# The half-swap of a rotary embedding: four ScalarE copies between partition groups in place of a matmul with a constant

## The reference

```
def _rotary(x, pos):
    half = x.shape[-1] // 2
    inv = ROPE_BASE ** (-jnp.arange(half, dtype=jnp.float32) / half)
    ang = pos.astype(jnp.float32)[:, None] * inv[None, :]
    cos = jnp.cos(ang)[None, :, None, :]
    sin = jnp.sin(ang)[None, :, None, :]
    xf = x.astype(jnp.float32)
    x1, x2 = xf[..., :half], xf[..., half:]
    return jnp.concatenate([x1 * cos - x2 * sin, x1 * sin + x2 * cos], axis=-1)
```

## Time and profile before

| | |
|---|---|
| median of the runs | 1412.16 us |
| profiled execution, device time | 1408.09 us |
| its span in the profile | 1406.3 us |
| PE busy | 1362.9 us, 97% of the span |
| DVE busy | 807.3 us, 57% |
| ACT busy | 625.0 us, 44% |
| POOL busy | 130.4 us, 9% |
| mean granted clock of PE | 0.992 |

### The profile page before, as it was taken

How to read it: one execution, slowest core, us unless ns; L and a number is a source line. 1 busy time by engine, 2 the same in 40 slices (tenths; PEclk the granted TensorE clock), 3 DMA queues, 4 the chain that set the end, 5 groups by cost and what they waited for, 6 DMA issues and landing times.

```text
span 1406.3 us, 24734 instructions
## 1 busy us (share of the span) xinstructions
PE 1362.9 (97%) x9649; PEld 1326.6 (94%) x9649; DVE 807.3 (57%) x1224; ACT 625.0 (44%) x987; POOL 130.4 (9%) x129
## 2 busy tenths in 40 slices
PE   6999999989999999999999999999899999999998
PEld 6999999978899999999999999999788999999998
DVE  4655544687655665564366555347865467555542
ACT  4444444552344554443454444346324455444333
POOL 2000000360000200000020000013500011000000
PEclk9999999999999999999999999999999999999999
DMA  5755555442233355545545554564322344555552
GB/s 154 204 165 164 161 159 155 139 108 77 79 113 102 103 155 149 149 142 149 153 116 149 148 150 147 148 175 112 86 78 84 98 120 123 149 149 149 149 145 72
DMA packets 351770, 187.34 MB, mean 133 GB/s; under 512 B 6316, under 2 KB 348600, under 8 KB 351704
## 3 DMA queue, kind: packets, MB, share of 16 engines
q1 hardware_dynamic: 348368, 177.49, 44.8%
q0 software_dynamic: 2496, 7.93, 1.6%
q10 hardware_dynamic: 840, 0.99, 0.3%
HBM read 182.07 MB, written 4.33 MB: 133 GB/s over the span
## 4 chain that ended last, share of the span: by engine, by line
PE 86%; DVE 6%; DMA 3%; ACT 2%; issue 1%; DVEq 1%; POOL 1%; ACTq 0%; SPq 0%; POOLq 0%
PE ps L616 26%; PE ps L617 26%; PE ps L618 26%; DVE w_l L495 2%; DVE scores L1423 1%; PE ps L905 1%; DMA raw<-in_w_in_dram 1%; PE ps L915 1%; DMA raw<-in_ffn_w_up_dram 1%; PE ps L804 1%; PE ps L926 1%; PE ps L672 1%; PE ps L679 1%; PE ps L879 1%; DMA raw<-in_w_out_dram 0%
## 5 line engine op out<-in xcount | busy, mean ns | idle before, releaser
L616 PE MATMUL ps<-xn_l,w_h 128*128 128x320 f32 x1840 | 579.9, 315 | 3.0 <-DVE xn_l L1260 2.0
L618 PE MATMUL ps<-xn_h,w_h 128*128 128x320 f32 x1840 | 569.2, 309 | 0.0
L617 PE MATMUL ps<-xn_h,w_l 128*128 128x320 f32 x1840 | 569.0, 309 | 0.0
L495 DVE TENSOR_TENSOR w_l<-raw,w_h 128x1024 fp32r<-128x1024 f32 (+1 forms) x340 | 408.3, 1203 | 181.9 <-ACT w_h L486 181.8
L486 ACT ACTIVATE w_h<-raw 128x1024 fp32r<-128x1024 f32 (+1 forms) x342 | 353.2, 1035 | 262.8 <-DMA raw<-in_ffn_w_down_dram 130.0
L616 PEld LDWEIGHTS ps<-xn_l,w_h 128*128 128x128 f32 x1840 | 346.4, 188 | 12.8 <-issue 3.6
L617 PEld LDWEIGHTS ps<-xn_h,w_l 128*128 128x128 f32 x1840 | 346.6, 188 | 0.7
L618 PEld LDWEIGHTS ps<-xn_h,w_h 128*128 128x128 f32 x1840 | 346.4, 188 | 0.0
L616 PE MATMUL ps<-hid_l,w_h 128*128 128x320 f32 x704 | 217.4, 309 | 0.0
L617 PE MATMUL ps<-hid_h,w_l 128*128 128x320 f32 x704 | 217.3, 309 | 0.0
L618 PE MATMUL ps<-hid_h,w_h 128*128 128x320 f32 x704 | 217.3, 309 | 0.0
(11 more groups left out here) (226 smaller groups left out, 1182.6 us busy)
## 6 DMA issues: line engine op xcount, KB each, us to landing
raw<-in_ffn_w_up_dram SPq DMA_DIRECT2D x176, 512.0 KB, 3.9
raw<-in_ffn_w_down_dram SPq DMA_DIRECT2D x64, 448.0 KB, 3.8
raw<-in_w_in_dram SPq DMA_DIRECT2D x54, 512.0 KB, 3.8
raw<-in_ffn_w_down_dram SPq DMA_DIRECT2D x32, 512.0 KB, 4.0
raw<-in_w_out_dram SPq DMA_DIRECT2D x16, 512.0 KB, 4.0
const<-in_tables_dram POOLq DMA_DIRECT2D x8, 272.0 KB, 4.4
x_in<-in_x_prompt_dram SPq DMA_DIRECT2D x1, 1024.0 KB, 3.8
scores<-in_cache_diff_k_dram POOLq DMA_DIRECT2D x2, 512.0 KB, 5.1
```

The source lines that it names most:

```text
L495: dve.tensor_tensor(w_l[s][:, 0:cols], raw[s][:, 0:cols], w_h[s][:, 0:cols], ALU.subtract).then_inc(w_lo, 1)
L616: pe.matmul(out, w_h[s][:, w], xl, start=first, stop=False)
L617: pe.matmul(out, w_l[s][:, w], xh, start=False, stop=False)
L618: return pe.matmul(out, w_h[s][:, w], xh, start=False, stop=last)
```

## The change

The constant matrix and the four matmuls per layer go. In their place ACT does four copies per tile in SBUF, each of 32 partitions and 320 columns, from one group of 32 partitions of `z` to the neighbouring group of `y[:, 7, :]`, two of them with the factor -1. DVE's first multiplication reads this tile of `y` (SBUF) instead of PSUM. As one tile of `y` serves all four, the copies of `rot` n wait for DVE's `rot` n - 1. PE's level 0 waits for `minus` instead of `rot1`, and bank 3 of PSUM is shared by two entries fewer.

```
-        elif kind in ("gla_o", "rot", "ret_s", "ret_o"):
+        elif kind == "rot":
+            act.append(f"turn{n}")
+            dve.append(f"rot{n}")
+        elif kind in ("gla_o", "ret_s", "ret_o"):
...
-    add("rot", rot)
...
-                        after(pe, l, "dve", "rot1")
+                        after(pe, l, "dve", "minus")
...
-                elif kind == "rot":
-                    pe.wait_ge(evac, l * GROUPS + G_MIX + RQ + n + 2)
-                    if n >= 2:
-                        shared_free(l, kind, n)
-                    else:
-                        after(pe, l, "act", "abs")
-                        after(pe, l, "dve", "minus")
-                    mark("pe", pe.matmul(ps[:, ROT_BANK[n], 0:T], C("rot"), z[:, RQ + n, :], start=True, stop=True), f"rot{n}")
...
+                elif kind == "rot":
+                    act.wait_ge(evac, l * GROUPS + G_MIX + RQ + n + 2)
+                    if n:
+                        after(act, l, "dve", f"rot{n - 1}")
+                    for g in (0, 64):
+                        act.activation(y[g:g + 32, 7, :], z[g + 32:g + 64, RQ + n, :], ACT.Copy, scale=-1.0)
+                        i = act.activation(y[g + 32:g + 64, 7, :], z[g:g + 32, RQ + n, :], ACT.Copy)
+                    mark("act", i, f"turn{n}")
...
-                    after(dve, l, "pe", f"rot{n}")
+                    after(dve, l, "act", f"turn{n}")
                     dve.drain()
-                    dve.tensor_tensor(t, ps[:, ROT_BANK[n], 0:T], C("sin"), ALU.mult)
+                    dve.tensor_tensor(t, t, C("sin"), ALU.mult)
```

More of the change, by code:

```diff
@@ L175 @@
 MILESTONES = milestones()
-READER = {"tok": ("act", "tok"), "rot": ("dve", "rot"), "ret_kt": ("act", "ret_kt"), "ketok": ("act", "ketok"), "ret_s": ("dve", "ret_s"),
+READER = {"tok": ("act", "tok"), "ret_kt": ("act", "ret_kt"), "ketok": ("act", "ketok"), "ret_s": ("dve", "ret_s"),
           "ret_state": ("dve", "ret_state"), "ret_o": ("dve", "ret_o"), "ret_mu": ("dve", "ret_xc")}
-SHARED = [(kind, "" if not arg else arg[0]) for kind, *arg in SCHEDULE if kind in READER and (kind, *arg) not in (("rot", 0), ("rot", 1))]
-ROT_BANK = (6, 7, 3, 3)
+SHARED = [(kind, "" if not arg else arg[0]) for kind, *arg in SCHEDULE if kind in READER]
 def constants():
@@ L260, in build @@
         NCONST = sum(n for _, n in table_at.values())
-        FIRST = table_at["rot"][0]
+        FIRST = table_at["cos"][0]
         N_PAR = 16 * 10
```

## The result

The kernel after takes 1423.55 us (median of 4 runs, 1421.76 to 1425.64). The kernel before took 1411.87 us beside it (4 runs, 1411.04 to 1413.54). The ratio is 1.0098, with a 95% interval of 1.0078 to 1.0119: slower. The ratio is estimated from the single executions; the two medians alone would give 1.0083. The profiled execution took 1421.76 us, with a span of 1420.0 us and a mean granted clock of 0.989. Before these were 1408.09, 1406.3 and 0.992.

The account below looks back on a forecast made before the run. Where `rot` 0 and 1 stand, it took engines to work in a circle led by DVE, not PE. 2 x (3.7 + 0.5) = 8.4 us on 1408.1 gives 1416.5; plus 4.1 for the timed median, 1420.6 us, range 1415.0 to 1425.0.

Parts of the forecast that it names:

- PE was the bound: Rival: PE leads, so all 4.3 us of removed matmuls come off, giving 1407.9 us; chance 0.06.
- level 1 on PE later: PE's level 1 waits for DVE's copy of level 0, delayed by ACT copies and POOL collisions: +4.0 us per layer.
- `rot` 2 gives back: At `rot` 2 DVE's 0.79 us wait for PE goes: -1.2 us per layer, between -0.7 and -1.4.
- `rot` 3: Late copies push `weight` 5 and POOL's `qk` 5 onto `rot` 3: +0.9 us per layer, between 0 and +1.
- sum without the clock: Level 1, `rot` 2 and `rot` 3 together: 4.0 - 1.2 + 0.9 = 3.7 us per layer.
- the clock: Granted clock falls after PE's wait before level 1, mostly covered by DVE: +0.5 us per layer, up to 2.0.
- clock low over two stages: Rival: the clock stays low over two stages, 2 x (3.7 + 2.0) = 11.4 us, so 1423.6 us; chance 0.20.
- Cheap copies: Rival: ACT copies on 32 partitions cost 0.15 us apiece, leaving +1.0 us per layer, 1414.2 us; chance 0.12.

Follow-up runs that it names:

- Experiment 1: Kernel before with only `rot` 0 and 1 turned by ACT copies, `rot` 2 and 3 still matmuls: 1420.39 us, ratio 1.0088.
- experiment 2: Kernel before with only `rot` 2 and 3 turned by ACT copies, sharing one tile of `y`: 1417.18 us, ratio 1.0048.
- experiment 7: Kernel after with other forms of the four copies, half-swap left out, only to read the distances between copies: 1426.86 us in its single execution.
- experiment 3: Kernel after plus dummy matmuls on PE ahead of levels 0, 1 and 5, results unread: 1415.70 us, ratio 1.0046.
- experiment 5: Kernel before with only `rot` 2 and 3 on ACT, their copies going to two tiles of `y` in turn: 1411.45 us, ratio 1.0002.
- experiment 10: Kernel after with two tiles of `y` in turn and dummy matmuls ahead of levels 0, 1 and 5: 1417.39 us, ratio 1.0048.
- experiment 9: Kernel after with two tiles of `y` in turn and dummy matmuls ahead of levels 0 and 1 alone: 1423.72 us, ratio 1.0102.
- experiment 11: Kernel before with the `rot` 2 matmul moved behind level 0 and `rot` 3 on ACT with its own tile: 1411.55 us, ratio 1.0020.
- experiment 6: Kernel before with only `rot` 2 and 3 on ACT, copied into PSUM bank 3 instead of SBUF: 1413.98 us, ratio 1.0020.
- experiment 4: Kernel after with one 128x320 ACT copy per rotation in place of four, swap and sign left out: 1411.40 us, ratio 1.0018.

## Why the prediction was right and where it failed

**The direction and the place: right, and shown.** I forecast slower, with 84 chances in 100, by PE waiting at level 1 for a DVE made late by ACT. The trace has the wait of 2.91 us there for DVE's copy of level 0. Experiment 1 carries this loss alone, and experiment 2 is at -0.02 up to level 2. The rival "PE was the bound" is out: its 4.3 us of matmuls went, and only the 0.7 us for which DVE had waited at `rot` 2 came back.

**The size: too small.** I forecast +8.4 us. The medians stand 11.7 us apart; the ratio of 1.0098 makes it 13.8 us, or 1426.0 us on the scale of the forecast, past the 1425.0 at which my range ended. That end was too low by its own terms: it took `rot` 2 at -1.3 beside the worst of all others, where its bound of -0.7 gives 4.9 + 2.0 = 6.9 us per layer, 1426.0 us. And it held no second fall of the clock.

**The terms of the sum,** in us per layer:

| step | forecast | measured |
|---|---|---|
| level 1 on PE later | +4.0 | +3.98 and +3.99 |
| `rot` 2 gives back | -1.2 | -0.8 (clock at 1.00) to -1.1 |
| `rot` 3 | +0.9 | +0.87 and +0.89 (clock at 1.00) |
| sum without the clock | +3.7 | +4.08 |
| the clock | +0.5 | +3.6 and +1.0 |
| both layers | +8.4 | +12.7 |

- **Level 1** came out to the hundredth, but by two errors that offset each other. The four copies cost 1.94 us and not 1.5; "I take 0.37 us of ACT per copy" was wrong, since I carried over an overlap from operations that follow each other on the same partitions (experiment 7). `rot` 1 is +4.52 us late, not +3.6. In return the collisions cost DVE less. I had 3.05 us undisturbed from `rot` 1 to the copy of level 0 and had added 1.9 for collisions; it took 4.00. POOL's product did begin 0.5 us behind `rot` 1 (298.70), as forecast, but only the sum gave way to it (1.42 us, as before). And where the next product met the `w_l`, it was POOL that was held, 2.52 us for a product that takes 1.55 to 1.58 elsewhere in this trace; the `w_l` took 1.36. I had charged both meetings to DVE, although the 2.27 us in the earlier trace rows were POOL's wait as well. That the two errors cancel is luck.
- **`rot` 2** gave back a little less than forecast. In the full change its operations do not meet POOL as hard as in experiment 2 (0.69 against 1.86 us for the first multiplication), so this term depends on where the others put it.
- **`rot` 3** has the right net value with a part of its cause overlooked. The `w_h` that waits for its weight tile is there (5.75 us; it starts at 310.84, which is 309.55 counted from the scan as before, near the 309 I gave). Behind it came the wait for `rot` 2 on the shared tile, which I had named in the change and had not priced: 1.93 us in the first layer, 0.43 at full clock in experiment 3. Level 4 is 1.7 us later than level 3; 0.9 of these come back before level 5: there a `w_l` of DVE took 2.10 us beside POOL in the kernel before, and takes 1.22 once POOL's product has moved away. Experiments 5 and 10 show the shared tile to cost 1.5 us with `rot` 0 and 1 on PE, and nothing in the full change, where the weight tile is late anyway.
- **The clock: the step that failed.** "I take 0.5 us per layer; nothing if the fall does not come, up to 2.0 if it lasts over level 2." I expected the fall at level 1, and that DVE's work would cover most of it. It cost 2.7 us at level 2 in the first layer (+6.70 against +3.97 in experiment 3) and 1.3 in the second. In the first layer the low clock lasted over the whole rest of unit 8 and over level 2, which took 1.38 us in place of 0.95. Then came a second fall that I had not foreseen at all, at level 5, after a wait of 3.19 us; `gla_state` in the first layer is +7.69 where level 5 was +6.53. In the second layer PE waited as long there and the clock held. Level 5 waited 1.45 us before (PE at 314.23); the lateness of `rot` 3 made it 3.2. Experiments 9 and 11 show this second fall by itself. The forecast stopped looking for waits behind level 1.

The rival "clock low over two stages", at 1423.6, is what the first layer did, and by the median the time came out at its value; I had given it 0.20. That does not make its mechanism complete: in it the low clock lasted from one fall, while here a second fall added to it. Cheap copies are out: a copy of 32 partitions takes what one of 128 takes.

By the ratios, experiment 3 puts the clock at 1.0098 less 1.0046, or 0.5% of 1411 us, about 7 us; the profiled execution gives 4.6. It is the shortest of the four, with a mean clock of 0.989; those of 1425.21 and 1425.64 us had 0.983 and 0.982. The intervals of the two ratios leave room for both values, and how often a fall comes over many executions stays open.

## What to carry to other kernels

Where engines hand work round in a circle, price an operation that is moved by its length on the engine that leads there, not by the load that the page's bound engine is freed of: 0.54 us of PE, for which DVE waited only at `rot` 2, was exchanged for 1.94 us of ACT, which the whole circle waited for at `rot` 0 and 1. Then follow the delay through every later wait of PE. In each one that grows the clock may fall (here it fell at waits from 1.56 to 3.19 us, and not at each of them), so price a fall where DVE will wait for the matmuls behind it, or fill the wait with matmuls that nobody reads, which here took the change from 1.0098 to 1.0046 of the kernel before.

## What the runs showed of the hardware that I had not expected

- ACT begins a copy of 320 columns 0.36 us after the one before it if both have the same source and destination partitions, and 0.48 us after it if either changes, at 32 or 64 partitions alike (experiment 7). Into PSUM the distance with changing partitions is 0.44 us (experiment 6).
- The length of PE's wait does not tell whether the clock falls. It fell behind waits of 1.56 us (experiment 6, with a stop of 0.86 us just ahead), 2.16 us (experiment 2) and 2.73 us (experiment 1), and stayed at 1.00 behind 2.26 us (experiment 4) and 2.73 us (level 0 of the kernel after). Before level 5, PE of the kernel after waited 3.19 us in the first layer and the granted clock went to 0.50; it waited 3.18 us in the second and the clock stayed at 1.00. Here is the second:

```profile
1020.93 0.95 PE L800 MATMUL ps<-sq 32*128 32x128 f32 x24 [3.18 <-DVE scores L1419]
...
1022.00:1025.00 3.00, 2.73 (x29) 2.50 (x31) 2.31 (x3) 0.10 (x1) 1.67 (x1) 1.00 0.00 0
```

- Taking a DVE operand out of SBUF spares that operation, not the next one: 0.49 and 1.45 us in place of 1.86 and 1.00 (experiments 6 and 2).
